# The last block of a two-layer decoder trunk: the second token block's sums made in two column halves, and the final norm rearranged

## The reference

```python
x = x + conv_ffn(h, ffn_w_gate[i], ffn_w_up[i], ffn_dw[i], ffn_dw_b[i], ffn_w_down[i])   # i = 1, last
return rms_norm(x, norm_final)

def conv_ffn(x, w_gate, w_up, dw, dw_b, w_down):
    g = causal_dwconv(x @ w_gate, dw, dw_b)
    return (jax.nn.silu(g) * (x @ w_up)) @ w_down

def rms_norm(x, g):
    y = xf * lax.rsqrt(jnp.mean(xf * xf, axis=-1, keepdims=True) + RMS_EPS)
    return y.astype(x.dtype) * g
```

## Time and profile before

| | |
|---|---|
| median of 3 runs | 2135.8 us (2135.8 to 2137.21) |
| the profiled execution's own time | 2136.06 us |
| its span, first to last instruction | 2134.1 us |
| TensorE busy | 2122.1 us, 99% |
| VectorE busy | 1449.4 us, 68% |
| ScalarE busy | 1056.7 us, 50% |
| mean granted TensorE clock | 0.999 of full |
| HBM read | 396.11 MB, 187 GB/s over the span |

### The profile page before, as it was taken

The page is one execution under the profiler, slowest core; times in us unless marked ns, Lnnn a source line. Parts: engine busy times, 40 slices in busy tenths (PEclk is TensorE's granted clock), DMA queues, the critical chain, the costliest instruction groups (busy, mean ns, idle before and its releaser), DMA issues.

```text
span 2134.1 us, 30450 instructions
## 1 busy us (share of the span) xinstructions
PE 2122.1 (99%) x10989; PEld 1807.2 (85%) x10989; DVE 1449.4 (68%) x2142; ACT 1056.7 (50%) x1507; POOL 47.7 (2%) x50
## 2 busy tenths in 40 slices
PE   9999999999999999999999999999999999999998
PEld 7888788888888888888888888888888888888887
DVE  6667757777777774454788867567777777764444
ACT  7545755544444444444544444554444544444443
POOL 0000000000000007000000000000000000000000
PEclk9999999999999999999999999999999999999999
DMA  8555456666666665555666554566666666656553
GB/s 301 198 186 182 158 178 184 190 188 186 194 182 194 183 192 192 192 192 186 184 175 173 182 178 142 194 180 194 181 194 187 186 191 184 195 192 214 195 193 114
DMA packets 513964, 399.27 MB, mean 187 GB/s; under 512 B 6606, under 2 KB 425896, under 8 KB 513552
## 3 DMA queue, kind: packets, MB, share of 16 engines
q1 hardware_dynamic: 513712, 398.15, 60.3%
q10 hardware_dynamic: 192, 0.28, 0.0%
HBM read 396.11 MB, written 2.10 MB: 187 GB/s over the span
## 4 chain that ended last, share of the span: by engine, by line
PE 97%; DMA 1%; DVE 1%; ACT 1%; SPq 0%; issue 0%; DVEq 0%; ACTq 0%
PE acc L1600 36%; PE acc L1605 18%; PE acc L1637 12%; PE acc L1638 12%; PE acc L1639 12%; PE acc L1982 1%; PE acc L1980 1%; PE acc L1981 1%; DMA sb_stage<-in_conv_w_in 1%; PE aux L1693 0%; PE aux L1991 0%; PE aux L1939 0%; PE aux L1764 0%; PE aux L1765 0%; PE aux L1766 0%
## 5 line engine op out<-in xcount | busy, mean ns | idle before, releaser
L947 DVE TENSOR_TENSOR sb_w_lo<-sb_stage,sb_w_hi 128x1024 fp32r<-128x1024 f32 (+1 forms) x743 | 902.9, 1218 | 512.1 <-ACT sb_w_hi L573 508.7
L573 ACT ACTIVATE sb_w_hi<-sb_stage 128x1024 fp32r<-128x1024 f32 (+1 forms) x743 | 780.4, 1053 | 654.9 <-PE acc L1639 369.7
L1600 PE MATMUL acc<-sb_normed,sb_w_hi 128*128 128x512 f32 x3264 | 1027.4, 396 | 0.0
L1605 PEld LDWEIGHTS acc<-sb_normed,sb_w_lo 128*128 128x128 f32 x3264 | 613.1, 188 | 144.9
L1605 PE MATMUL acc<-sb_normed,sb_w_lo 128*128 128x256 f32 x3264 | 641.4, 278 | 0.0
L1600 PEld LDWEIGHTS acc<-sb_normed,sb_w_hi 128*128 128x128 f32 x3264 | 497.7, 189 | 0.6
L1637 PE MATMUL acc<-sb_w_hi,sb_hidden 128*128 128x512 f32 x674 | 262.5, 389 | 0.0
L1639 PE MATMUL acc<-sb_w_hi,sb_hidden 128*128 128x512 f32 x674 | 262.2, 389 | 0.0
L1638 PE MATMUL acc<-sb_w_lo,sb_hidden 128*128 128x512 f32 x674 | 262.2, 389 | 0.0
L585 ACT ACTIVATE sb_corr<-acc 128x256 f32<-128x256 f32 x204 | 77.0, 377 | 210.7 <-PE acc L1605 210.6
L1639 PEld LDWEIGHTS acc<-sb_w_hi,sb_hidden 128*128 128x128 f32 x674 | 126.5, 188 | 26.4
(11 more groups left out here) (236 smaller groups left out, 1640.7 us busy)
## 6 DMA issues: line engine op xcount, KB each, us to landing
sb_stage<-in_ffn_w_gate SPq DMA_DIRECT2D x86, 1024.0 KB, 5.5
sb_stage<-in_ffn_w_up SPq DMA_DIRECT2D x86, 1024.0 KB, 5.5
sb_stage<-in_ffn_w_down SPq DMA_DIRECT2D x80, 1024.0 KB, 5.0
sb_stage<-in_attn_w_qkv SPq DMA_DIRECT2D x48, 1024.0 KB, 5.4
sb_stage<-in_conv_w_in SPq DMA_DIRECT2D x30, 1024.0 KB, 5.7
sb_stage<-in_conv_w_out SPq DMA_DIRECT2D x16, 1024.0 KB, 5.1
sb_stage<-in_attn_w_o SPq DMA_DIRECT2D x16, 1024.0 KB, 5.0
sb_stage<-in_ffn_w_down SPq DMA_DIRECT2D x8, 768.0 KB, 4.3
```

The costliest lines, as they stand in the source:

```text
L573: nc.scalar.activation(w_hi[:, (2 * first + h) % PIECES, 0:size], stage[:, first % STAGES, off:off + size], ACT.Copy).then_inc(hi_ready, 1)
L947: nc.vector.tensor_tensor(w_lo[:, slot, 0:size], stage[:, first % STAGES, off:off + size], w_hi[:, slot, 0:size].bitcast(F32), ALU.subtrac ...
L1600: nc.tensor.matmul(acc[:, bank, :], w_hi[:, slot, q * P:(q + 1) * P], operand[:, k, :], start=begin, stop=False, skip_group_check=True)
L1605: return nc.tensor.matmul(acc[:, bank, T:2 * T], w_lo[:, slot, q * P:(q + 1) * P], operand[:, k, 0:T], start=False, stop=end, skip_group_c ...
```

## The change

For token block 1, `rows_first` leaves out the last weight block, and a new function `last_halves` does its three tiles in two passes of 256 columns: the left half (columns 1536 to 1791 of the output) into the same bank as before, then the right half (from `EDGE` on) into a bank of `aux` that starts at zero.

```diff
+                            if (name, b, at) == ("down1", TB - 1, end):
+                                continue
...
+            def last_halves(at):
+
+                c, j = ORDER["down1"][at]
+                n, half = B["down1"] + at, WIDE // 2
+                bank = (C["down1"] + TB * c + TB - 1) % BANKS
+                for edge, sums in ((0, acc[:, bank, 0:half]), (half, aux[:, 0, 0:half])):
+                    for h in range(2):
+                        slot = (2 * n + h) % PIECES
+                        for q in range(columns(n)[h] // WIDE):
+                            k = KB * j + KB // 2 * h + q
+                            part = slice(WIDE * q + edge, WIDE * q + edge + half)
+                            high, low = hidden[:, k, P:T], hidden[:, k, T + P:2 * T]
+                            begin = edge > 0 and h + q == 0
+                            nc.tensor.matmul(sums, high, w_hi[:, slot, part], start=begin, stop=False)
+                            nc.tensor.matmul(sums, high, w_lo[:, slot, part], start=False, stop=False)
+                            ins = nc.tensor.matmul(sums, low, w_hi[:, slot, part], start=False, stop=k == KF - 1)
+                        if edge:
+                            ins.then_inc(pieces_done, 1)
+                    if edge == 0:
+                        ins.then_inc(rows_done, 1)
```

```diff
             last_rows(1)
-            last_scale(1)
+            dve.wait_ge(evacuated, BANKS + C["down1"] + TB * CH)
+            last_gain(slice(D - WIDE, EDGE))
+            dve.wait_ge(pieces_done, 2 * (B["down1"] + CH * ND))
+            cols = resid[:, 1, EDGE:D]
+            nc.vector.tensor_tensor(cols, aux[:, 0, 0:D - EDGE], cols, ALU.add).then_inc(tail_added, 1)
+            own.mark(last_parts(1))
+            own.wait()
+            nc.vector.tensor_scalar(sq_tail[:, 1:2], sq_sum[:, n, 1:2], 1.0 / D, RMS_EPS, ALU.mult,
+                                    ALU.add).then_inc(sq_ready, 1)
+            dve.wait_ge(tail_added, 1)
+            last_gain(slice(EDGE, D))
+            last_root(1)
+            own.wait()
+            own.done()
+            nc.vector.tensor_scalar(resid[:, 1, D - WIDE:D], gained_tail, row_scale[:, n, 1:2], None,
+                                    ALU.mult).then_inc(tail_scaled[1], 1)
             dve.wait_ge(gained, TB * (CH - 1))
-            dve.wait_ge(rms_ready, n + 2)
-            rows = resid[:, 1, 0:D - 2 * WIDE]
+            rows = resid[:, 1, 0:LEFT]
             nc.vector.tensor_scalar(rows, rows, row_scale[:, n, 1:2], None, ALU.mult).then_inc(row_scaled[1], 1)
-            last_tail(1)
```

```diff
+            def last_gain(cols):
+
+                own.mark(nc.vector.tensor_tensor(gained_tail[:, cols.start - D + WIDE:cols.stop - D + WIDE],
+                                                 resid[:, 1, cols], gain_rows[:, cols], ALU.mult))
```

ScalarE squares the halves apart, takes the root with the bias, scales columns 768 to 1535 (`LEFT` = 768) and issues the store for them itself:

```diff
+            last_square(1, slice(D - WIDE, EDGE), sq_parts[:, n, 1, CH - 1:CH])
+            act.wait_ge(tail_added, 1)
+            act.wait_ge(squared, TB * (CH * n + CH - 1) + 2)
+            last_square(1, slice(EDGE, D), sq_tail[:, 0:1])
+            act.wait_ge(squared, TB * (CH * n + CH - 1) + 3)
+            act.wait_ge(sq_ready, n + 2)
+            nc.scalar.activation(row_scale[:, n, 1:2], sq_tail[:, 0:1], ACT.Sqrt, bias=sq_tail[:, 1:2],
+                                 scale=1.0 / D).then_inc(root_ready, 1)
+            act.wait_ge(rms_ready, len(STAT) + 1)
+            rows = resid[:, 1, LEFT:D - WIDE]
+            nc.scalar.activation(rows, rows, ACT.Copy, scale=row_scale[:, n, 1:2]).then_inc(third_scaled, 1)
+            act.wait_ge(third_scaled, 1)
+            act.dma_start(out[0][P:T, LEFT:D - WIDE], rows).then_inc(stored, 16)
```

SyncE is left with two stores for token block 1, and the two columns of the new tile `sq_tail` are taken from the unused tile `edge`, so that what lies behind keeps its address:

```diff
-                      (1, third_scaled, slice(D - 2 * WIDE, D - WIDE)), (1, row_scaled[1], slice(0, D - 2 * WIDE)),
-                      (1, tail_scaled[1], slice(D - WIDE, D)))
+                      (1, tail_scaled[1], slice(D - WIDE, D)), (1, row_scaled[1], slice(0, LEFT)))
...
-        sb("edge", [P, 8])
+        sq_tail = sb("sq_tail", [P, 2])
+        sb("edge", [P, 6])
```

More of the change, by code:

```diff
@@ L337, in trunk @@
         third_scaled = sem("third_scaled")
+        tail_added = sem("tail_added")
         tail_scaled = [sem(f"tail_scaled{b}") for b in range(TB)]
@@ L918, in _ @@
             n = STAT["down1"]
[L919 to L935, removed]
@@ new lines, in last_square @@
+            def last_square(b, cols, part):
+                nc.scalar.activation(square[:, 0:cols.stop - cols.start], resid[:, b, cols], ACT.Square,
+                                     accum_out=part).then_inc(squared, 1)
+            act.wait_ge(evacuated, BANKS + C["down1"] + TB * (CH - 1) + 1)
+            act.wait_ge(squared, TB * (CH * n + CH - 1))
+            last_square(0, slice(D - WIDE, D), sq_parts[:, n, 0, CH - 1:CH])
+            act.wait_ge(sq_ready, n + 1)
+            nc.scalar.activation(row_scale[:, n, 0:1], sq_sum[:, n, 0:1], ACT.Sqrt, bias=const[:, 0:1],
+                                 scale=1.0 / D).then_inc(root_ready, 1)
@@ new lines, in _ @@
+            act.wait_ge(rms_ready, len(STAT))
+            act.wait_ge(gained, TB * (CH - 1))
+            rows = resid[:, 0, 0:D - WIDE]
+            nc.scalar.activation(rows, rows, ACT.Copy, scale=row_scale[:, n, 0:1]).then_inc(row_scaled[0], 1)
+            act.wait_ge(evacuated, BANKS + C["down1"] + TB * CH)
+            act.wait_ge(squared, TB * (CH * n + CH - 1) + 1)
+            last_square(1, slice(D - WIDE, EDGE), sq_parts[:, n, 1, CH - 1:CH])
+            act.wait_ge(tail_added, 1)
+            act.wait_ge(squared, TB * (CH * n + CH - 1) + 2)
@@ L1536, in _ @@
             n = STAT["down1"]
+            own.turn(0, 3)
             def last_rows(b):
[L1540 to L1543, removed]
+                dve.wait_ge(rows_done, 2 + b)
                 cols = resid[:, b, D - WIDE:D]
@@ L1552, in last_scale, with last_root, last_parts @@
+            def last_root(b):
                 dve.wait_ge(root_ready, n + b + 1)
                 nc.vector.reciprocal(row_scale[:, n, b:b + 1], row_scale[:, n, b:b + 1]).then_inc(rms_ready, 1)
[L1555 removed]
                 dve.wait_ge(rms_ready, n + b + 1)
[L1558 to L1561 removed]
+            def last_parts(b):
+                dve.wait_ge(squared, TB * (CH * n + CH - 1) + b + 1)
+                return nc.vector.tensor_reduce(sq_sum[:, n, b:b + 1], sq_parts[:, n, b, :], AX.X, ALU.add)
@@ L1563, in _ @@
             last_rows(0)
-            last_scale(0)
-            last_tail(0)
-            last_rows(1)
-            last_scale(1)
+            last_parts(0).then_inc(sq_ready, 1)
+            last_root(0)
+            cols = resid[:, 0, D - WIDE:D]
+            nc.vector.scalar_tensor_tensor(out=cols, in0=cols, scalar=row_scale[:, n, 0:1],
+                                           in1=gain_rows[:, D - WIDE:D], op0=ALU.mult,
+                                           op1=ALU.mult).then_inc(tail_scaled[0], 1)
```

10 lines of the change are left out of this document (5 added, 5 removed).

## The result

The changed kernel takes 2155.24 us (median of 6 runs, 2154.28 to 2155.54), the kernel before 2136.22 (6 runs, 2135.8 to 2137.21): a ratio of 1.0087 [1.0077, 1.0097]. It is **19 us slower**; the prediction was 2135.2, with 2137.0 as the upper end. The loss is not where the change was made.

A forecast was written before the change was run, and what follows sets the result against it. TensorE was taken as the bound, busy 99% of the span, so only the tail behind its last matmul counts. Tail terms sum to -0.64 us: 2136.06 becomes 2135.4, less 0.26 for the median, said as 2135.2; range 2134.0 to 2137.0.

The forecast's parts named there:

- everything ahead of the tail: All instructions before the last weight block: same on all five engines, buffers at the same addresses, so no time added.
- Case D: Something outside the tail, such as instruction fetching or code placement: chance 0.07, over 4.3 us slower 0.04, faster 0.03.
- The step of the short matmuls: Last block on TensorE: eighteen matmuls of 256 columns start every 0.117 us, ending 0.07 us later than before.
- Rival C: Last block: weight loads set the 256-column matmuls' step; 0.19 gives 2136.3 us (chance 0.07), 0.31 gives 2138.4 (0.03).
- The wait of the add: VectorE's right-half add, queued behind the multiplication ahead, starts 0.12 us behind TensorE's end, not 0.04: +0.08.
- The sum of the tail: From the last block's matmuls to the first of the last stores: all changes together save 0.64 us.
- the square: ScalarE's square of the right half in the tail: 0.51 us with the accumulator read instead of 0.73, -0.22.
- from there to the root: From the square's end to the root: the reduce leaves the path, 0.06 us instead of 0.22, -0.16.
- to the first scaled columns behind the reciprocal: VectorE's first scaling in the tail: 0.10 wait plus 0.51 us from the reciprocal's end, not 0.74, -0.13.
- an engine's wait for its own result: Tail chain: an engine needing its own previous result waits 0.06 to 0.10 us before starting.
- rival B: Last stores: ScalarE's store on a second queue lands 0.6 us or more late, cancelling the gain; 2135.8 us, chance 0.15.
- first store plus 3.85: End of the kernel: the last store lands 3.85 us after the first of the last stores is issued.

## Why the prediction was wrong

**What failed** is the term for everything ahead of the tail, put at nothing by one sentence: "the buffers keep their addresses (two columns go from a filler to the new tile), so I put nothing on it". It was read from the source, where 2 + 6 columns stand for 8. In the built program both tiles are rounded up to 32 bytes, the tiles behind move by 32, and 2742 matmuls cost 6.8 ns more each. Nor would knowing of the move have been enough, since no row of before gives it a price. Only the runs do: 19.2 us for the move alone (2155.85 against 2136.66), and none without it (2136.11 against 2136.66). Case D named "another placement" of the code only, with 0.04 for slower, and no price.

**The step of the short matmuls** was right: (2145.80 - 2143.78)/17 = 0.119 us, 0.117 said. Rival C fell. The weight load that starts with the first of them, at 2143.78, takes 0.19 and lies beside it, and the next matmul starts at 2143.90. The Trainium skill ("TensorE: Matmul & The Clock Gate", section "The mechanism") says in one sentence that loads overlap matmuls in flight only where the row group differs; by that sentence, with all rows in every load, the steps would be 0.31, and eighteen of them say otherwise. The same section also names a background weight buffer as the target of a load that is pulled ahead, and that sentence the trace does not contradict.

**The wait of the add** was over-priced. I had it 0.12 behind TensorE's end; TensorE ends at 2145.80 + 0.28 = 2146.08 and the add's record starts at 2146.12, 0.04 behind it, the same as in the kernel before (2126.89 against 2126.85). The profile's chain goes through VectorE instead: the left half's add (0.70), the multiplication (0.42) and the right half's add, one behind the other from 2145.05 on. But the add starts 0.34 after the multiplication, about the pace of VectorE without a wait (the instruction behind the add starts 0.33 after it), so both it and TensorE let the add go at about the same moment (in the kernel without the filler the add starts at 2127.18, 0.35 behind the multiplication and 0.04 behind TensorE's end). Which of them holds it is not shown; that the multiplication in the way costs anything is not either.

**The sum of the tail** was -0.64 and is -0.81. By its terms, said and measured: TensorE's end +0.07, +0.10 (2.30 from the first matmul, 2.20 before); the start of the add +0.08, 0.00; the add -0.28, -0.28 (from TensorE's end to the add's end 0.46 for 0.74); the square -0.22, -0.21 (0.52 with its read); from there to the root -0.16, -0.20, and to the first scaled columns behind the reciprocal -0.13, -0.22. Most of the difference is one mistake, made three times: I priced an engine's wait for its own result at 0.06 to 0.10 from a pair of rows of before, and the three in the chain (the multiplication behind the left half's add, the root behind the square, the scaling behind the reciprocal) took 0.02 to 0.04. The scaling took 0.49, for 0.51 said.

**The stores** (rival B) did not take it back: ScalarE issues in 0.38 us and its 384 KB land in 3.1. The rule "first store plus 3.85" gave 3.93. With the filler out the kernel lies at 2136.11, inside the range, and the gain of the tail, 0.55 by the medians, is about as small as forecast and cannot be told from none.

**What stays open**: why the distance counts. That two reads of the same memory, one for the operand that streams and one for the next weights, get into each other's way at some distances would fit; nothing here shows it. Nor is it known why the down stages are fastest at 0, 256 and 512 bytes while the up stages gain from +32 and +64, or why `w_lo` alone slows the steps of `w_hi`, in the up stages too, or why the two widths of the up stages do not go together.

## What to carry to other kernels

Before writing "the buffers stay put", compare the address of every tile in the two built programs: sizes are rounded up, so a tile split in two takes more. On a kernel that TensorE bounds, the distances between the operands can be worth more (19 us here) than a chain behind the last matmul (0.8 us), so keep them when a tile is added, and try some offsets for each kind of stage. When a small edit moves the time by much, compare first the mean duration of equal instructions far away from it.

## What the runs showed of the hardware

- A matmul of 512 columns in the down stages steps by 0.2257 us where `hidden` and both weight tiles lie multiples of 256 bytes apart, and by 0.2326 at 32 bytes more; 32, 64, 96 and 128 bytes cost 19, 19, 21 and 16 us of the kernel, 256 and 512 nothing. With `w_lo` alone 32 bytes further the steps of `w_hi` are slower too, and the kernel loses 36 us.
- In the up stages, 512 and 256 columns in turn, the stream at +32 and +64 bytes makes the kernel 5.2 and 9.5 us faster (about half a microsecond of each is the tail), at +128 it changes nothing, and at +224 it is 7.6 slower.
- With every tile 32 bytes further the loads of 1 MB land in 5.9 us instead of 5.5.
- Matmuls of 256 columns follow each other every 0.119 us, with a full weight load of 0.19 before each.
- VectorE's and ScalarE's waits for a result of their own took 0.02 to 0.04 us in the changed kernel's tail.
